# Where the on-chip tiles of a two-layer hybrid decoder trunk begin

## The reference

```
h = rms_norm(x, norm_w[layer])
proj = h @ w_in[layer]
y = concat(gla(...), sliding_window_attention(...), differential_attention(...), rglru(...))
x = x + (y * silu(gate)) @ w_out[layer]
```

## The kernel before

| tile | bytes | start mod 2048, before | after the change |
|---|---|---|---|
| `act` | 65,536 | 128 | 0 |
| `act_T` | 32,768 | 128 | 0 |
| `mix_Y` | 32,896 | 128 | 0 |
| `w_raw`, `w_hi`, `w_lo` | 16,384, 16,384, 12,288 | 256 | 0 |
| `stage`, `wa` | 4,096 each | 256 | 0 |
| `ident` and the three tiles behind it | 512 each | 256, 768, 1280, 1792 | 0, 512, 1024, 1536 |
| `mix` | 17,408 | 1952 | 0 |

## Time and profile before

### The profile page before, as it was taken

The page is one execution under the profiler, slowest core; times in us unless marked ns, Lnnn a source line. Parts: engine busy times, 40 slices in busy tenths (PEclk is TensorE's granted clock), DMA queues, the critical chain, the costliest instruction groups (busy, mean ns, idle before and its releaser), DMA issues.

```text
span 3024.1 us, 37606 instructions
## 1 busy us (share of the span) xinstructions
PE 2984.7 (99%) x14857; PEld 2480.8 (82%) x14857; DVE 1606.0 (53%) x2120; ACT 1458.7 (48%) x2059; POOL 52.8 (2%) x107
## 2 busy tenths in 40 slices
PE   8999999999999999999999999999999999999999
PEld 6778898888887898877878788988888787987877
DVE  5445456555666446444554445555556664554444
ACT  5344445545556455444543434445455665553333
POOL 2000000000000000000000000000000000000000
PEclk9999999999999999999999999999999999999999
DMA  7565556666555666666656655566655555666664
GB/s 225 168 184 158 160 163 178 177 182 177 174 161 163 179 180 193 209 209 198 207 172 187 180 155 165 164 178 178 179 174 174 160 167 174 187 197 201 216 213 163
DMA packets 281889, 546.68 MB, mean 181 GB/s; under 512 B 17688, under 2 KB 21920, under 8 KB 281712
## 3 DMA queue, kind: packets, MB, share of 16 engines
q1 hardware_dynamic: 271472, 524.88, 57.6%
q0 software_dynamic: 5552, 17.26, 1.9%
q10 hardware_dynamic: 4688, 2.13, 0.3%
HBM read 535.81 MB, written 8.39 MB: 180 GB/s over the span
## 4 chain that ended last, share of the span: by engine, by line
PE 98%; DMA 1%; ACT 1%; issue 1%; DVE 0%; ACTq 0%; PEldq 0%; DVEq 0%
PE main L1139 92%; PE mixer L1139 5%; DMA w_raw<-in_w_in 1%; ACT L383 0%; PE mixer L1353 0%; PE mixer L1198 0%; ACT stage L383 0%; PE mixer L1293 0%; PE mixer L1333 0%; PE mixer L1186 0%; DMA mix<-in_norm_w 0%; PE mixer L1321 0%; PE mixer L1283 0%; PE mixer L1320 0%; DVE w_lo L690 0%
## 5 line engine op out<-in xcount | busy, mean ns | idle before, releaser
L1139 PE MATMUL main<-w_hi,act 128*128 128x512 f32 x6912 | 2238.7, 399 | 26.4 <-PE main L1139 13.2
L690 DVE TENSOR_TENSOR w_lo<-w_raw,w_hi 128x1024 fp32r<-128x1024 f32 x992 | 1213.8, 1225 | 1281.0 <-PE main L1139 1045.6
L376 ACT ACTIVATE w_hi<-w_raw 128x1024 fp32r<-128x1024 f32 x992 | 1044.5, 1059 | 1138.1 <-PE main L1139 1123.1
L1139 PEld LDWEIGHTS main<-w_hi,act 128*128 128x128 f32 x6912 | 1302.8, 188 | 343.4 <-issue 39.6
L1139 PE MATMUL main<-w_lo,act 128*128 128x512 f32 x3456 | 1364.3, 395 | 0.0
L1139 PEld LDWEIGHTS main<-w_lo,act 128*128 128x128 f32 x3456 | 652.3, 189 | 143.4
L1139 PE MATMUL main<-act,w_hi 128*128 128x256 f32 x2048 | 373.7, 283 | 3.5 <-PE main L1139 1.8
L1139 PEld LDWEIGHTS main<-act,w_hi 128*128 128x128 f32 x2048 | 316.8, 188 | 6.2 <-issue 5.8
L1139 PE MATMUL main<-act,w_lo 128*128 128x256 f32 x1024 | 288.2, 281 | 0.0
L1139 PEld LDWEIGHTS main<-act,w_lo 128*128 128x128 f32 x1024 | 192.9, 188 | 0.2
L670 DVE SCALAR_TENSOR_TENSOR act<-act_T,par,act 128x256 fp32r<-128x256 f32 x96 | 42.0, 480 | 2.8 <-ACT act L358 2.5
(11 more groups left out here) (250 smaller groups left out, 1126.4 us busy)
## 6 DMA issues: line engine op xcount, KB each, us to landing
w_raw<-in_w_in SPq DMA_DIRECT2D x736, 512.0 KB, 3.6
w_raw<-in_w_out SPq DMA_DIRECT2D x256, 512.0 KB, 3.6
out<-mix POOLq DMA_DIRECT2D x15, 512.0 KB, 3.3
mix<-in_x POOLq DMA_DIRECT2D x8, 512.0 KB, 5.9
mix<-out POOLq DMA_DIRECT2D x8, 512.0 KB, 5.8
mix_Y<-in_x SPq DMA_DIRECT2D x3, 1024.0 KB, 16.6
mix_Y<-in_x SPq DMA_DIRECT2D x2, 512.0 KB, 5.0
act_T<-in_lru_w_r ACTq DMA_DIRECT2D x16, 64.0 KB, 1.9
```

The lines of the kernel that those rows point to most:

```text
L376: act.activation(w_hi[:, n % HI, :, :], w_raw[:, n % RAW, :, :], ACT.Copy).then_inc(w_hi_ready, 1)
L690: dve.tensor_tensor(w_lo[:, n % LO, :, :], w_raw[:, n % RAW, :, :], w_hi[:, n % HI, :, :].bitcast(F32), ALU.subtract).then_inc(w_lo_ready, 1)
L1139: return pe.matmul(out_, lhsT, rhs, start=start, stop=stop, skip_group_check=True)
```

## The change

Six small tiles are declared ahead of `act` and a tile `pad` that nothing reads or writes follows them, 1,920 bytes together with the rounding to 32. A second unused tile `pad2` of 1,920 bytes stands between `mix_Y` and `w_raw`. Six of the small tiles leave the place behind the constants where they stood. The last tile ends at byte 228,352 of 229,344. No instruction, loop, wait, queue or size of a transfer is touched; only the addresses of the operands are others.

```
+        chunk1 = sb("chunk1", [P, 2])
+        par = sb("par", [P, DEPTH, NQ])
+        rstd = sb("rstd", [P, T])
+        ssq = sb("ssq", [P, T, 8])
+        small = sb("small", [P, 64])
+        cst = sb("cst", [P, 4])
+        pad = sb("pad", [P, 56])
         A = sb("act", [P, KT, 2, SEQ], F32R)
         F = sb("act_T", [P, KT * SEQ])
         YB = sb("mix_Y", [P, 6 * BW + HEADS * (SEQ + 4)])
+        pad2 = sb("pad2", [P, 480])
         w_raw = sb("w_raw", [P, RAW, KG, NC])
         w_hi = sb("w_hi", [P, HI, KG, NC], F32R)
         w_lo = sb("w_lo", [P, LO, KG, NC], F32R)
...
         ones = sb("ones", [P, P])
-        chunk1 = sb("chunk1", [P, 2])
         dist = sb("dist", [P, 3 * P])
         dist_swa = sb("dist_swa", [P, 3 * P])
-        par = sb("par", [P, DEPTH, NQ])
-        rstd = sb("rstd", [P, T])
         rstd_row = sb("rstd_row", [P, SEQ])
-        ssq = sb("ssq", [P, T, 8])
-        small = sb("small", [P, 64])
-        cst = sb("cst", [P, 4])
```

## The result

The changed kernel takes 2978.95 us, median of 4 (2978.37 to 2979.48); the kernel before takes 3026.85 us, median of 4 too (3026.21 to 3027.89). The ratio is 0.9841, 95% interval 0.9824 to 0.9858: 47.9 us or 1.6% faster, far outside the forecast of no change and its range.

The account below looks back on a forecast made before the run. TensorE's distance between matmul starts was taken to bound the kernel; every part of the change was taken as zero, so 3025.8 us plus nothing, with the median 0.5 us above, gave 3026.3 us, range 3021 to 3032.

Parts of the forecast that it names:

- What bounds the kernel: TensorE's distance between matmul starts sets the end: 98% of the chain of waits is TensorE, DMA has 1%.
- The streamed operand: Weight streams crossing a multiple of 2048 bytes: a crossing bounded at 0.01 us per matmul, 104 us over 10,368; taken as nothing.
- The surplus argument: F32R streams' surplus, 17.5 ns (512 columns) and 10.6 (256), mostly grows with columns; better starts give at most 3.7 ns each, 50 us.
- the sum: The profiled execution's 3025.8 us plus nothing from any part; forecast 3026.3 us, as the median lies 0.5 us higher.
- The stationary operand: Loads of 128 columns of `act`: hi and lo have the same 188 ns median and hide behind 232.5 ns streams; zero.
- The collision rival: Weights and `act` both starting at 0, loads meet streams at equal low address bits: up to 78 us slower, 3104 us; chance 4%.
- The rival of a fixed part: One cost per stream, at most 3.7 ns on 13,440 streams, goes away: 50 us less, 2976 us; chance 5%.
- theory A: From the experiments: a streamed operand that crosses a multiple of 2048 bytes pays one fixed cost; 226.7 ns only at Y = 0.
- The mixers, ScalarE, VectorE and the transfers: Other operands' new starts: zero each; bounds 1.5 us for the mixers and 0.4 us for transfers at the start.
- The "margin": F32R streams take 17.5 ns (512 columns) and 10.6 ns (256) more than mixers' streams of half as many columns.
- The chances: No change within 0.2% 84%, faster 9%, slower 7%; surplus going with the odd starts, 2812 us, 3%.

Follow-up runs that it names:

- the sweep: TensorE alone, model left out, 52 segments varying tile starts, columns loaded, stream length and plain float32; 512-column streams took 226.7 ns in phase, 233.3 at a difference of 128.

## Why the prediction was wrong

**What bounds the kernel** was right: TensorE's distance between starts set the time, everything else kept its duration to 1%, but for the loads of the turned products (188 to 192 ns, still hidden), and 46.3 of the 46.4 us are TensorE's.

**The streamed operand** was right for what it looked at and missed what mattered. Crossing a multiple of 2048 costs nothing: the rings at 1024 are as fast. But the earlier trace rows compare part 0 and part 1 of `act`, 1024 bytes apart, both at the same phase to the weights modulo 256. No row of before could show a cost of the phase, because every pair of operands of the big products had the same phase, 128.

**The surplus argument is the step that failed**, and with it the zero that the sum had for TensorE's step. I read that most of the surplus grows with the columns, which the sweep confirms, and concluded that the start could not be its cause, since a start is paid once per stream. The growing part is the one that the phase decides: 57.3 against 53.3 ns per 128 columns. The 3.7 ns that I took as the most that an address could give had been worked out from two steps that were both out of phase; the fixed part in phase is 13 ns and is still there after the change. What went was 5.6 ns of each step in a whole chunk, 48.2 us over the streams of 512 columns, for which the sum had nothing.

**The stationary operand**: loads hide behind the stream and kept their 188 ns beside the long streams, so the row was right and beside the point. Taking zero for it was wrong: with the weight rings left at 256, moving `act` and the tiles beside it to 0 brought the whole gain (2978.97 us). A load's duration does not show this; the step does.

**The collision rival** named the right quantity, the phase between the two operands, and had the wrong sign and the wrong test. I set its price at +78 us; in phase is the fast case for long streams, -48 us, and the slow one for turned streams, +5 us. The four places of a load within a block, which I took for four phases, are 512 bytes apart and so one phase modulo 256. The rows that I leaned on the earlier trace rows could not tell.

**The rival of a fixed part**, 2976 us at 5%, comes within 3 us of the result by another mechanism. That agreement is chance: theory A, its like in the experiments, fell.

**The mixers, ScalarE, VectorE and the transfers** were right. The mean of L692 moved by 1 ns and the mixers' matmuls read plain float32, which does not notice the phase. The wait for weights at the start went from 18.19 to 18.48 us. The "margin" over the mixers' 215 ns compared unlike things: each plain float32 matmul of the code is two of those instructions, so their step says nothing on how fast an F32R stream can go.

**The chances** were too sure. That "no such stream begins at a multiple of 512 bytes in this kernel, so a fully even start is untried" was a reason to leave the question open, and I gave it 3%.

The Trainium skill ("SBUF — State Buffer", section "Who interferes with whom") gives TensorE two independent read ports and says that it never waits on anyone. These runs agree as far as other engines go, since the steps are nearly the same with all others at rest (226.7 ns in phase and 232.3 to 233.3 at 128) as in the kernels (227.1, and 232.5 to 233.4). Between TensorE's own two reads the measurement decides: the distance of their addresses changes the step from 226.7 to 234.2 ns. Why the distance does this, no run shows.

## What to carry to other kernels

Where a profile shows 98% TensorE and F32R operands, compare the distance between starts with the columns at full clock (512 at 2.4 GHz are 213 ns), and sweep the byte distance between the stationary and the streamed tile modulo 256 with TensorE alone: one kernel of some 30 segments shows it, and the rest of the program can be left out. Streams of 384 and 512 columns wanted equal phase here, with both starts at multiples of 32, and the saving was 1.6% for a line of unused bytes; streams of 256 columns wanted another, so a tile that serves in both roles is a compromise or needs a shift per role. When all rows of a trace share one value of a quantity, they say nothing on that quantity, however many there are.

## What the runs showed of the hardware that was not expected

- The step of a 512-column F32R stream goes from 226.7 ns (difference 0) over 229.0 (192) to 233.3 (64, 128) and 234.2 (start 128 against 32), with no other engine at work. With the weights at 0, `act` at 16 and 240 is as fast as at 0; both at 16 or 48 is not (230.0 and 233.3).
- Turned streams of 256 columns take 120.0 ns in phase, 118.7 at 128, and at 64 one of two steps, 113.3 or 117.8 ns, picked by what ran before; at 192 the kernel shows 113.6 and 117.9.
- A weight load of 32 columns in place of 128 does not shorten a 512-column step: 231.6 ns in phase against 226.7. With loads under 128 columns the phase of 128 costs at most 1.7 ns, with 128 columns 6.6.
- After an interruption steps of 0.23 to 0.24 us come first: in the changed kernel for all 12 matmuls of the group at 1249.9 us, for some seven of the stretch at 1253.1.
